# Gate/up weight halves followed one by one from landing to reuse, with the down rows asked for between them

## The reference, cut to what matters

```python
def swiglu(x, wg, wu, wd):
    return (jax.nn.silu(x @ wg) * (x @ wu)) @ wd          # 1024 -> 2816 -> 1024

def moe_swiglu(x, router, wg, wu, wd):                    # 8 experts, top 2
    ...
    for e in range(N_EXPERTS):
        out = out + gates[:, e:e + 1] * swiglu(xt, wg[e], wu[e], wd[e])
```

## Time and profile before

| | |
|---|---|
| time, median of 3 runs | 2539.93 us |
| the 3 runs | 2542.61, 2531.61, 2539.93 us |
| profiled execution: device time | 2543.85 us |
| profiled execution: span of the trace | 2542.0 us |
| PE busy | 2480.9 us, 98% of the span |
| DVE busy | 1769.5 us, 70% |
| ACT busy | 1397.0 us, 55% |
| mean granted TensorE clock | 0.998 |
| read from HBM | 588.09 MB, 234 GB/s over the span |
| DMA share in the expert layer | about 0.9, some 360 GB/s |

### The profile page before, as it was taken

The page is one execution under the profiler, slowest core; times in us unless marked ns, Lnnn a source line. Parts: engine busy times, 40 slices in busy tenths (PEclk is TensorE's granted clock), DMA queues, the critical chain, the costliest instruction groups (busy, mean ns, idle before and its releaser), DMA issues.

```text
span 2542.0 us, 32402 instructions
## 1 busy us (share of the span) xinstructions
PE 2480.9 (98%) x11877; PEld 2033.2 (80%) x11877; DVE 1769.5 (70%) x1750; ACT 1397.0 (55%) x1524; POOL 245.4 (10%) x317
## 2 busy tenths in 40 slices
PE   8899999999999999999999999999999999999998
PEld 7778877877787888887788888878888888887887
DVE  4764557788888989989855567786465555778554
ACT  4544444676777777777644455544444445454533
POOL 3000021000000000000141103010004200300000
PEclk9999999999999999999999999999999999999999
DMA  7355444798998999999785444355548634435551
GB/s 272 117 219 195 182 136 155 282 358 346 358 367 348 362 366 355 375 354 350 265 269 208 157 172 154 142 201 205 192 154 251 231 142 182 166 138 197 196 191 66
DMA packets 89577, 595.83 MB, mean 234 GB/s; under 512 B 11616, under 2 KB 11760, under 8 KB 22016
## 3 DMA queue, kind: packets, MB, share of 16 engines
q1 hardware_dynamic: 77760, 558.99, 57.9%
q0 software_dynamic: 11712, 35.43, 5.0%
HBM read 588.09 MB, written 6.29 MB: 234 GB/s over the span
## 4 chain that ended last, share of the span: by engine, by line
PE 74%; DVE 11%; DMA 5%; ACT 4%; issue 4%; POOL 1%; SPq 0%; DVEq 0%; ACTq 0%; POOLq 0%
PE pp L659 16%; PE pp L661 16%; PE pp L660 16%; PE acc L659 6%; PE acc L661 6%; PE acc L660 6%; DMA raw_a<-in_moe_gu 2%; DVE lo_a L2782 2%; DMA raw_b<-in_moe_wd 2%; PE tp L899 2%; DVE lo_a L2264 1%; ACT hi_a L1637 1%; PE acc L1039 1%; PE tp L671 1%; ACT hi_a L1576 1%
## 5 line engine op out<-in xcount | busy, mean ns | idle before, releaser
L659 PE MATMUL pp<-hi_a,uT_hi 128*128 128x512 f32 (+1 forms) x2140 | 852.9, 399 | 5.2 <-DVE rows L2274 1.4
L661 PE MATMUL pp<-hi_a,uT_lo 128*128 128x512 f32 (+1 forms) x2140 | 832.7, 389 | 0.0
L660 PE MATMUL pp<-lo_a,uT_hi 128*128 128x512 f32 (+1 forms) x2140 | 830.8, 388 | 0.0
L2264 DVE TENSOR_TENSOR lo_a<-raw_a,hi_a 128x2048 fp32r<-128x2048 f32 x282 | 650.1, 2306 | 136.4 <-ACT hi_a L1637 135.6
L1637 ACT ACTIVATE hi_a<-raw_a 128x2048 fp32r<-128x2048 f32 x282 | 537.9, 1909 | 40.3 <-DMA raw_a<-in_moe_gu 39.9
L659 PEld LDWEIGHTS pp<-hi_a,uT_hi 128*128 128x128 f32 x2140 | 402.4, 188 | 87.0 <-issue 5.9
L661 PEld LDWEIGHTS pp<-hi_a,uT_lo 128*128 128x128 f32 x2140 | 402.0, 188 | 85.9
L660 PEld LDWEIGHTS pp<-lo_a,uT_hi 128*128 128x128 f32 x2140 | 403.1, 188 | 76.5
L660 PE MATMUL acc<-lo_b,hT_hi 128*128 128x512 f32 x792 | 308.2, 389 | 0.0
L2301 DVE TENSOR_TENSOR lo_b<-raw_b,hi_b 128x2048 fp32r<-128x2048 f32 x115 | 263.4, 2291 | 42.9 <-ACT hi_b L1660 42.1
L659 PE MATMUL acc<-hi_b,hT_hi 128*128 128x512 f32 x572 | 224.5, 392 | 6.8 <-DVE lo_b L2301 6.7
(11 more groups left out here) (303 smaller groups left out, 2730.3 us busy)
## 6 DMA issues: line engine op xcount, KB each, us to landing
raw_a<-in_moe_gu SPq DMA_DIRECT2D x176, 1024.0 KB, 6.7
raw_a<-in_ffn_w_gu SPq DMA_DIRECT2D x88, 1024.0 KB, 6.5
raw_b<-in_moe_wd SPq DMA_DIRECT2D x87, 1024.0 KB, 8.6
raw_a<-in_w_in SPq DMA_DIRECT2D x70, 1024.0 KB, 6.8
raw_b<-in_ffn_w_down SPq DMA_DIRECT2D x44, 1024.0 KB, 4.9
raw_a<-in_ffn_gu SPq DMA_DIRECT2D x22, 1024.0 KB, 6.7
raw_a<-in_w_out SPq DMA_DIRECT2D x16, 1024.0 KB, 5.9
raw_a<-in_w_branch SPq DMA_DIRECT2D x12, 1024.0 KB, 6.1
```

The source lines that it names most:

```text
L659: nc.tensor.matmul(out_ap, l_hi, r_hi, start=start, stop=False, skip_group_check=True)
L660: nc.tensor.matmul(out_ap, l_hi, r_lo, start=False, stop=False, skip_group_check=True)
L661: return nc.tensor.matmul(out_ap, l_lo, r_hi, start=False, stop=stop, skip_group_check=True)
L2264: ins = nc.vector.tensor_tensor(lo_a[:, slot, cs], raw_a[:, slot, cs], hi_a[:, slot, cs].bitcast(F32), ALU.subtract)
```

## The change

Each slot of `raw_a` has two landing semaphores now, `s_al` for its first half and `s_al2` for its second. ACT waits for each half just before it copies it, everywhere (`hi_chunk_a`, which copies both at once, waits for both). In the expert layer, and only there, DVE signals a new semaphore `s_alofront` when the low part of a first half is made. SP then asks for the first half of that slot; next comes its wait for PE and the down rows; then its wait for `s_alo` and the second half. The dense layers keep the old order of requests.

```diff
                 for j in range(2):
                     cs = slice(j * w // 2, (j + 1) * w // 2)
-                    sp.dma_start(raw_a[:, slot, cs], src[:, cs]).then_inc(s_al[slot], 16)
+                    sp.dma_start(raw_a[:, slot, cs], src[:, cs]).then_inc((s_al, s_al2)[j][slot], 16)
...
-            def gate_up(weights, slot, e, j):
+            def gate_up(weights, slot, e, j, parts=(0, 1)):
-                for g in range(2):
+                for g in parts:
                     sp.dma_start(raw_a[:, slot, g * 2048:(g + 1) * 2048],
                                  weights[0][bass.ds(e * P, P), bass.ds(j * 4096 + g * 2048, 2048)]) \
-                      .then_inc(s_al[slot], 16)
+                      .then_inc((s_al, s_al2)[g][slot], 16)
...
+                def sides(c, ea, ja, eb, jb):
+                    if experts == 1:
+                        side_a(c, ea, ja)
+                        side_b(c, eb, jb)
+                        return
+                    sp.wait_ge(s_alofront, c.at(1))
+                    gate_up(weights, (a0 + c.rest) % 2, ea, ja, (0,))
+                    side_b(c, eb, jb)
+                    sp.wait_ge(s_alo, c.at(a0 + 1))
+                    gate_up(weights, (a0 + c.rest) % 2, ea, ja, (1,))
...
-                            side_a(Chunk(i + half, odd + r), e, i * 2 + (r + 2))
-                            side_b(Chunk(i + half, odd + r), e, i * 2 + r)
+                            sides(Chunk(i + half, odd + r), e, i * 2 + (r + 2), e, i * 2 + r)
...
                 if 0 in parts:
-                    landed[slot] += 32
-                    act.wait_ge(s_al[slot], landed[slot])
+                    landed[slot] += 16
                 for part in parts:
+                    act.wait_ge((s_al, s_al2)[part][slot], landed[slot] - (16, 0)[part])
...
-                    if part == 0:
-                        act.wait_ge(s_al[slot], c.turns(0) * 32 + (base[slot] + 32))
+                    act.wait_ge((s_al, s_al2)[part][slot], c.turns(0) * 16 + (base[slot] + 16 * part))
...
                     if part:
                         ins.then_inc(s_alo, 1)
+                    elif experts > 1:
+                        ins.then_inc(s_alofront, 1)
```

More of the change, by code:

```diff
@@ L317, in program @@
         s_al = [sem("s_al0"), sem("s_al1")]
+        s_al2 = [sem("s_al20"), sem("s_al21")]
+        s_alofront = sem("s_alofront")
         s_bl = [sem("s_bl0"), sem("s_bl1")]
@@ L527, in _ @@
                 cs = slice(1024 * q, 1024 * (q + 1))
-                sp.dma_start(raw_a[:, 0, cs], a["w_in"][0][:, cs]).then_inc(s_early[q] if q < 3 else s_al[0], 16)
+                sp.dma_start(raw_a[:, 0, cs], a["w_in"][0][:, cs]).then_inc(s_early[q] if q < 3 else s_al2[0], 16)
             sp.dma_start(x[:, 1, :], a["x"][0, P:2 * P, :]).then_inc(s_xin[1], 16)
@@ L532, in _ @@
                              a["w_in"][0][:, KD * 512 + 2048 * h:KD * 512 + 2048 * (h + 1)]) \
-                  .then_inc((s_early[3], s_al[1])[h], 16)
+                  .then_inc((s_early[3], s_al2[1])[h], 16)
             n["a"] = 2
@@ L586, in expert @@
                         for r in range(2):
-                            side_a(Chunk(i + half, odd + r), e, i * 2 + (r + 2))
-                            side_b(Chunk(i + half, odd + r), e, i * 2 + r)
-                    side_a(Chunk(half + 4, odd), e, N_FCH - 1)
-                    side_b(Chunk(half + 4, odd), e, N_FCH - 3)
+                            sides(Chunk(i + half, odd + r), e, i * 2 + (r + 2), e, i * 2 + r)
+                    sides(Chunk(half + 4, odd), e, N_FCH - 1, e, N_FCH - 3)
                     if last:
@@ L601, in expert @@
                         if not last:
-                            side_a(c, e + 1, r)
-                        elif ahead:
+                            sides(c, e + 1, r, e, N_FCH - 2 + r)
+                            continue
+                        if ahead:
                             ahead(r)
@@ L1531, in _ @@
             n = Tally()
-            landed = [-16, -16]
+            landed = [0, 0]
             n["b"], n["bu"] = 1, 2
@@ L1539, in hi_chunk_a @@
                 slot = n["a"] % 2
-                landed[slot] += 32
-                act.wait_ge(s_al[slot], landed[slot])
+                landed[slot] += 16
+                act.wait_ge(s_al[slot], landed[slot] - 16)
+                act.wait_ge(s_al2[slot], landed[slot])
                 if freed:
@@ L1722, in ffn @@
                 for c in range(k):
-                    landed[(a1 + c) % 2] += 32
+                    landed[(a1 + c) % 2] += 16
                     if experts == 1 or c + 1 < k:
@@ L2011, in _ @@
             hi_tile(0)
-            landed[0] += 32
+            landed[0] += 16
             n["a"] += 1
@@ L2015, in _ @@
                 cs = slice(1024 * q, 1024 * (q + 1))
-                act.wait_ge(*((s_early[q], 16) if q < 3 else (s_al[0], landed[0])))
+                act.wait_ge(*((s_early[q], 16) if q < 3 else (s_al2[0], landed[0])))
                 nc.scalar.activation(hi_a[:, 0, cs], raw_a[:, 0, cs], ACT.Copy) \
@@ L2021, in _ @@
                 if i == 0:
-                    landed[1] += 32
+                    landed[1] += 16
                     n["a"] += 1
@@ L2025, in _ @@
                         cs = slice(2048 * h, 2048 * (h + 1))
-                        act.wait_ge(*((s_early[3], 16), (s_al[1], landed[1]))[h])
+                        act.wait_ge(*((s_early[3], 16), (s_al2[1], landed[1]))[h])
                         nc.scalar.activation(hi_a[:, 1, cs], raw_a[:, 1, cs], ACT.Copy) \
@@ L2162, in lo_turned, with lo_halves @@
                                         hT_hi[:, :, ts].bitcast(F32), ALU.subtract).then_inc(s_tlo, 1)
-            def lo_halves(size=4096, parts=(0, 1)):
+            def lo_halves(size=4096, parts=(0, 1), front=None):
                 if 0 in parts:
@@ L2176, in lo_halves @@
                         ins.then_inc(s_alo, 1)
+                    elif front:
+                        ins.then_inc(front, 1)
             def gain():
@@ L3021, in _ @@
                     signal(s_ppv)
-                    lo_halves(4096, (0,))
+                    lo_halves(4096, (0,), s_alofront)
                     gathered_opening((0,))
```

## The result

The changed kernel took **2592.95 us** (median of 6 runs, 2586.93 to 2595.0) against 2540.7 us for the kernel before (6 runs). The ratio is 1.0196, with a 95% interval of 1.018 to 1.0212: 2% slower, where the forecast was 2528.5 us and the range ended at 2539.

A forecast was written before the change was run, and what follows sets the result against it. PE, busy 98% of the span, was taken to bound the kernel, with gaps from late expert weights. Gains of 12.5 us there and 2.5 at the start, together 15.0, took 2543.85 to 2528.9, set at 2528.5 us; range 2521 to 2539.

The forecast's parts named there:

- First half asked for at its own low part: Expert layer: SP asks at 756.4, 0.3 us after DVE's low part; lands about 764.2, wanted 768.7, 4.5 us to spare.
- Down rows "at 754.44, where PE's down product puts it": Expert layer: down rows, requested ahead of the second half, land at 759.2, wanted at 763.2; 4.0 us to spare, before 0.1.
- the second half "at 754.9": Expert layer: asked for behind SP's wait for PE, not at 753.6; lands 761.7, wanted 765.0, 3.3 us to spare.
- The spare times of 4.5, 4.0 and 3.3 us: Expert layer, quiet round: margins between landing and use for first half, down rows and second half; thinnest before was 0.1.
- the layer: Expert layer: fewer late weights gain 12.5 us, 85% of an upper end of 14.7; lower end 7.3.
- the start: First projection's third chunk: separate waits for halves bring queries' copy to 28.1 and may keep the clock; 2.5 us, 1.8 to 3.5.
- The second half comes too late: Rival, expert layer: second half, hanging on PE through SP's wait, lands 4 us late; 2573 us, slower; chance 0.08.
- The laggard is a rate: Rival, expert layer: one DMA engine needs 9.5 us every slow round, so margin lasts three rounds; 2534 us; chance 0.18.
- DVE is next: Rival, expert layer: DVE's extra steps at expert changes cause slow rounds, so only the start gains; 2537 us; chance 0.12.

## Why the prediction was wrong

**The step that failed is the first one, "First half asked for at its own low part".** It read the wait `s_alofront, c.at(1)` as the low part of the chunk that holds the slot and put the request 0.3 us behind DVE's 756.09. In the kernel as it runs, the request comes one chunk later, and a steady round takes 9.35 us in place of 8.42. The order of instructions on SP, which the prediction rested on, was right: the wait stands where it was said to stand. What it doesn't show is which signal satisfies the wait. That needs the signals counted from the start of the layer, and the first expert chunk gives none. The instruction waited for the low part of the next chunk. Had the first chunk's signals been counted, the rest was in reach from rows that the prediction used: 4.7 + 1.9 + 2.3 + 0.3 = 9.2 us for a loop that has to close in 8.42.

**The steps behind it fell with it.** Down rows "at 754.44, where PE's down product puts it" and the second half "at 754.9" assumed that SP waits for PE there. In after it never does, since all three go out in one group. The spare times of 4.5, 4.0 and 3.3 us were for requests that went out most of a round earlier.

**The sizes held where the mechanism was as described.** With the count mended the kernel takes 2527.7 us against the forecast of 2528.5, and experts 95.8 to 96.0 against 95.9 to 97. The spare times held as well: in the expert layer of that kernel a first half lands 4.7 us before its copy, the down rows 4.1 and a second half 3.4 (medians of 82 rounds), where the prediction had 4.5, 4.0 and 3.3. The least were 1.8, 1.3 and 0.5, so in the worst rounds hardly any margin was left. The second half asked for at 744.97, for one, landed 8.2 us later, at 753.2, for a copy at 754.88: 1.7 us. The nearness of the total is in part luck. In the profiled executions the layer gained 14.9 us (771.2 to 756.4, first to last silu) and not 12.5, the start 1.8 and not 2.5, together 16.4 of span and not 15.0. What the prediction did not see is that order or early request alone would bring the same gain.

**The start was right in after.** ACT's second copy at 26.31, then the copy of queries and keys at the predicted time, and the two stretches of the earlier trace rows:

```profile
26.31 1.91 ACT L1591 ACTIVATE hi_a<-raw_a 128x2048 fp32r<-128x2048 f32 x1 [3.18 <-DMA raw_a<-in_w_in]
28.12 0.58 ACT L1800 ACTIVATE qkT<-tp 128x512 f32<-128x512 f32 x1
```

```profile
27.60:30.50 2.90, 1.74 (x12) 1.28 (x13) 2.25 (x2) 1.59 (x3) 0.00 (x0) 1.00 1.02 421
30.50:34.30 3.80, 3.51 (x18) 2.60 (x17) 1.69 (x5) 1.48 (x5) 2.12 (x3) 1.00 1.02 372
```

The granted clock there is 1.00, where it was 0.55, and the expert layer began 2.3 us earlier (forecast 2.5, from 1.8 to 3.5). The 2.3 us are one execution's; the last section says why they can't be taken for granted.

**The rivals.** *The second half comes too late* had the right sign and even nearly the right size (2573) by a wrong way: it was to hang on PE, and PE held nothing up; its chance of 0.08 was for a mechanism that didn't act. *The laggard is a rate* fell: it would have left long experts once its margin was used up, and the experts of three kernels are all at 95.8 to 96.0. *DVE is next* fell by the same rows; DVE is at 87.4 of 95.9 us and binds nothing. The rival "the change doesn't do what it says" was missing, and it is the one that came.

**What stays open.** Why one DMA engine fell behind in some rounds of before was not settled. Second halves that land late are still there with the count mended (9.7 us at most, 6.7 at the median, much like the 9.5 and 6.7 of before). The runs show only that they cost nothing once requests stand in time or in the order of use, with a landing for each half. The new order without the early request, and the early request in the old order, were not run with one landing for both halves.

## What to carry to other kernels

When a wait gets a semaphore of its own, count its signals from the first one: find every place that produced the old signal, those ahead of the loop above all, and check that the first wait is met by the instruction that it means; in a trace, the first request of the stage shows it (here 458.6 against 439.3 at the latest). A count that is one behind did not stop the program here; it cost a loop: request, landing, copy and release must then close in one round and not in two, and the sum of their durations against the round says at once that it will cost, and roughly how much. Put requests in the order in which they are used, or send them early, and let each be waited for alone. Here separate waits with neither of the two only moved the lateness, and both of the two without separate waits made the kernel slower.

## What the runs showed of the hardware

**The dips of the granted clock move.** In the window from 30.5 to 34.3 us before had 0.55, and after and all kernels with separate landings had 1.00. But their dips are elsewhere. Three of them have one from 446 to 456 us (separate landings alone, the early request in the old order, and the shared landing), and the kernel with the count mended has two shorter ones in the first 120 us. From 446 to 456 us, first the kernel with separate landings alone (with the 6 us ahead of it), then the one with separate landings and the new order:

```profile
440.00:446.00 6.00, 5.69 (x49) 5.14 (x48) 5.26 (x11) 3.17 (x5) 0.86 (x2) 0.99 0.62 259
446.00:456.00 10.00, 10.00 (x50) 10.00 (x49) 5.97 (x14) 6.86 (x7) 2.22 (x4) 0.50 0.67 211
```

```profile
440.00:446.00 6.00, 5.69 (x48) 5.29 (x48) 5.47 (x12) 3.35 (x5) 0.86 (x2) 1.00 0.71 298
446.00:456.00 10.00, 9.35 (x81) 8.67 (x80) 8.24 (x22) 7.24 (x7) 2.23 (x4) 1.00 0.63 211
```

50 matmuls against 81 in the same 10 us: 0.50 is the level of 1.2 GHz. PE was busy for 5.69 of the 6 us ahead in both, so it was not idle before the clock fell. PE, ACT and DVE have the same instructions up to there in both, and the expert layer began at 467.63 in the one and at 464.04 in the other. So some 3.6 us hang on where the clock falls, which is more than the whole start term. Each kernel has one profile, and why the clock falls there in some of them was not settled.

**A PE that waited long in each round lost its clock too.** In the kernel of one more chunk late PE had 5 to 6 us of gaps a round, and the mean granted clock of the program was 0.937 against 0.998 before; in one stretch of the layer (one profile of one execution):

```profile
780.00:800.00 20.00, 14.85 (x50) 11.49 (x49) 10.83 (x8) 7.19 (x6) 0.00 (x0) 0.77 0.47 178
```

In after, where PE's gaps were near 1 us a round, it stayed at 1.00.
